# A decoder block on one core: x also laid out by features, the first norm's factors applied where projections leave PSUM, the front's weights laid out piece by piece

## The reference

```
xn   = x * rsqrt(mean(x*x, features) + 1e-6) * g_mix        # RMSNorm, one factor per token
proj = xn @ w_in     # q,k,v of attention A (4 x 128 columns each), q of B, six k/v groups of B
                     # (kcr, vcr, ks, vs, kw, vw: 128 columns each), 24 head gates, 2 x 1024 merge gates
# kcr and vcr: blocks of 32 tokens at stride 16 (31 of them), plus positions, flattened,
#              then gelu(. @ w1 + b1) @ w2  -> compressed keys and values
out1 = x + merge(attention_A, attention_B, gates) @ w_out
```

## Time and profile before

| | us |
|---|---|
| median of 3 executions | 1177.87 (1176.14 to 1178.73) |
| profiled execution | 1176.71 |
| its span, first to last instruction | 1174.9 |
| PE busy in the span | 1109.4 (94%) |
| DVE, ACT, POOL busy | 457.6, 286.4, 286.9 |

### The profile page before, as it was taken

The page is one execution under the profiler, slowest core; times in us unless marked ns, Lnnn a source line. Parts: engine busy times, 40 slices in busy tenths (PEclk is TensorE's granted clock), DMA queues, the critical chain, the costliest instruction groups (busy, mean ns, idle before and its releaser), DMA issues.

```text
span 1174.9 us, 19004 instructions
## 1 busy us (share of the span) xinstructions
PE 1109.4 (94%) x7570; PEld 654.2 (56%) x7571; DVE 457.6 (39%) x1026; ACT 286.4 (24%) x642; POOL 286.9 (24%) x215
## 2 busy tenths in 40 slices
PE   6999999999998989989999999999998899989796
PEld 5888787767776879654333433334343333433375
DVE  5244655545446733542223421212221211111787
ACT  5123333333336510031111111111111111111523
POOL 5522524342333520010111111111111112110043
PEclk9999999999999989989999999999999989989898
DMA  9921222221213430669999999999999999998771
GB/s 297 241 54 37 73 55 73 55 54 54 56 37 111 123 118 37 251 248 413 406 420 415 421 422 424 418 410 419 407 420 405 407 408 406 405 396 315 311 315 71
DMA packets 118072, 305.67 MB, mean 260 GB/s; under 512 B 21688, under 2 KB 79712, under 8 KB 92128
## 3 DMA queue, kind: packets, MB, share of 16 engines
q1 hardware_dynamic: 105856, 270.88, 60.3%
q0 software_dynamic: 12128, 33.57, 7.2%
HBM read 288.69 MB, written 26.21 MB: 268 GB/s over the span
## 4 chain that ended last, share of the span: by engine, by line
PE 72%; DMA 9%; SPq 7%; issue 6%; DVE 2%; POOLq 1%; POOL 1%; ACT 1%; DVEq 0%; ACTq 0%
PE bank L1467 17%; PE bank L457 16%; PE bank L1491 8%; DMA sb_gate_up<-in_w_up 7%; SPq L988 5%; PE bank L1083 4%; PE bank L1073 4%; PE bank L466 3%; PE bank L490 3%; PE bank L521 3%; DMA sb_down<-in_w_down 3%; PE bank L1457 2%; PE bank L503 2%; PE bank L1108 2%; SPq L992 2%
## 5 line engine op out<-in xcount | busy, mean ns | idle before, releaser
L1467 PE MATMUL bank<-sb_gate_up,sb_xgT 128*32 128x512 f32 (+2 forms) x2144 | 304.9, 610 | 19.3 <-DMA sb_gate_up<-in_w_up 19.3
L1467 PEld LDWEIGHTS bank<-sb_gate_up,sb_xgT 128*32 128x32 f32 (+2 forms) x2144 | 96.2, 119 | 196.1 <-issue 193.0
L457 PE MATMUL bank<-sb_x_hl,sb_w_hl 128*128 128x512 f32 x768 | 189.1, 398 | 1.0 <-DVE sb_x_hl L578 1.0
L457 PEld LDWEIGHTS bank<-sb_x_hl,sb_w_hl 128*128 128x128 f32 x768 | 140.4, 188 | 47.6 <-issue 17.0
L1491 PE MATMUL bank<-sb_down,sb_work 128*32 128x512 f32 (+2 forms) x1072 | 153.0, 595 | 2.8 <-DMA sb_down<-in_w_down 1.6
L1549 POOL DMA_INDIRECT expert_rows<-sb_rows_out,sb_work x42 | 43.3, 1032 | 459.6 <-DVE sb_rows_out L1627 439.9
L241 POOL TENSOR_TENSOR sb_w_hl<-sb_r,sb_w_hl 128x1024 fp32r<-128x1024 f32 x54 | 131.2, 2432 | 59.7 <-ACT sb_w_hl L1196 45.0
L1637 DVE TENSOR_TENSOR sb_work<-sb_work,bank 128x256 f32<-128x256 f32 x42 | 17.7, 423 | 274.3 <-ACT sb_work L1673 274.3
L1491 PEld LDWEIGHTS bank<-sb_down,sb_work 128*32 128x32 f32 (+2 forms) x1072 | 46.5, 116 | 79.2 <-issue 76.5
L1673 ACT ACTIVATE sb_work<-bank 128x256 f32<-128x256 f32 x42 | 16.2, 386 | 302.7 <-PE bank L1467 302.7
L656 DVE CUSTOM_DVE_ANT_0 sb_h<-bank,sb_bias 128x128 f32<-128x128 f32 (+3 forms) x96 | 43.3, 488 | 112.3 <-PE bank L490 111.8
(11 more groups left out here) (258 smaller groups left out, 1324.7 us busy)
## 6 DMA issues: line engine op xcount, KB each, us to landing
sb_gate_up<-in_w_gate SPq DMA_DIRECT2D x64, 1024.0 KB, 19.8
sb_gate_up<-in_w_up SPq DMA_DIRECT2D x64, 1024.0 KB, 27.9
sb_down<-in_w_down SPq DMA_DIRECT2D x64, 1024.0 KB, 28.8
sb_r<-in_w_in SPq DMA_DIRECT2D x34, 512.0 KB, 3.8
sb_rows<-expert_rows SPq DMA_DIRECT2D x6, 2048.0 KB, 16.3
sb_r<-in_w_out SPq DMA_DIRECT2D x8, 512.0 KB, 3.7
sb_rows<-expert_rows SPq DMA_DIRECT2D x3, 1024.0 KB, 8.7
sb_h<-in_x SPq DMA_DIRECT2D x4, 512.0 KB, 5.2
```

Of the source, the lines that this page charges most:

```text
L457: last = nc.tensor.matmul(out[:, :], w6_hl[:, slot_at[n], zw, k, :], x_hl[:, zx, k, :], start=k + i == 0, stop=k == KD - 1 and i == 2)
L1467: last = nc.tensor.matmul(bank[BH][rows, :], xgT[:, k, rows], gate_up[slot_of[r]][:, :, k, :], start=k == 0, stop=k == KD - 1)
```

## The change

Nothing of the arithmetic on weights changes; the layouts are made ahead of the launch. x_T is x by features, [128, 4096]; w_front holds every piece as [128, 1024], so that a partition's part is one run of 4 KB; the compression weights, biases and positions come ready laid out too. x_hl is now made of x_T times g, without the tokens' factors, and each factor is applied at eviction: by rbc, the factors spread over 128 partitions (for products by features), or by rr (for products by rows). rbc comes from a product of ones with four diagonal blocks.

```diff
 front_sync:
-            for t in range(NT): ... h[:, t] <- x tile t (identity after t == 1)
-            load_columns 0, 1; biases, positions; load_columns 2 to 4
+            load_piece(sp, 0)
+            x_by_features(0)                  # y[:, c] <- x_T, 512 KB each
+            load_piece(sp, 1)
+            for c in range(1, NT):
+                x_by_features(c)
+            load_piece(sp, 2)
+            for t in range(NT):
+                sp.dma_start(h[:, t, :], a["x"][0, t * P:(t + 1) * P, :]).then_inc(s_x[t], 16)
+            sp.dma_start(cst[:, 0:2 * P], a["cst"][:, 0:2 * P]).then_inc(s_ident, 16)
+            for n in range(3, 5):
+                load_piece(sp, n)
             ... head gates' weights; then b1, pos2, pos2x; rest of the constants; pieces 5, 6; w1[0]; w2; piece 7; w1[1]; ...
 front_gpsimd:
-            pool.dma_start(g_rows, ...)
+            pool.dma_start(g_col, a["g_mix_col"][:, :]).then_inc(s_g, 16)
-            for t in range(NT): wait s_ms; rr[t] = ...      (ahead of all pieces)
             for n in range(N_ACT_HI):
                 pool.wait_ge(s_w_hi, n + 1)
                 rest_of_piece(buf_of[n], slot_at[n])
+                if n == 2:
+                    for t in range(NT):
+                        pool.wait_ge(s_ms, t + 1)
+                        nc.gpsimd.tensor_tensor(rr[:, t:t + 1], ms[:, t:t + 1], C["nhalf"][:, 0:1], ALU.pow).then_inc(s_rr, 1)
 front_tensor:
-            transposes of g_rows, of y (32), of pos_rows
-                if j == 0 and f >= 2: pe.wait_ge(F["evicted"], f - 1)
+                out = bank_of(f)              # banks 0, 1, 6, 7 for f < 4, then BF[f % 2]
+                if j == 0 and f >= 4:
+                    pe.wait_ge(F["evicted"], bank_before.get(f, f - 2) + 1)      # {4: 0, 5: 1}
+                    if (f, j) == (2, 1):
+                        pe.wait_ge(s_ident, 16)
+                        pe.wait_ge(s_diag, 1)
+                        for t in range(NT):
+                            last = nc.tensor.matmul(bank[BS[0]][:, t * P:(t + 1) * P], C["ones"], diag[:, t, :], start=True, stop=True)
+                        last.then_inc(s_rbc, 1)
 front_vector:
+            dve.wait_ge(s_g, 16)
+            for k in range(KD):
+                dve.wait_ge(s_x_T[k // 2], 16)
+                dve.wait_ge(s_hi, k + 1)
+                nc.vector.scalar_tensor_tensor(out=x_hl[:, 1, k, :], in0=x_T[:, k, :], scalar=g_col[:, k:k + 1], in1=x_hl[:, 0, k, :].bitcast(F32), ...)
             for t in range(NT): norm_sums of h[:, t]        (now behind the low halves)
+            for t in range(NT):
+                dve.wait_ge(s_rr, t + 1)
+                last = nc.vector.tensor_scalar(diag[:, t, :], ident, rr[:, t:t + 1], None, ALU.mult)
+            last.then_inc(s_diag, 1)
+            dve.wait_ge(s_rbc, 1)
+            nc.vector.tensor_copy(rbc, bank[BS[0]][:, :])
 compress_blocks(i):
-                raw_kv = bank[BF[i]][:, :].rearrange("p (n t two) -> p two t n", t=8, two=2)
+                nc.vector.tensor_tensor(kv_normed[i], bank_of(i)[:, :], rbc, ALU.mult)
+                dve.drain()
+                raw_kv = kv_normed[i].rearrange("p (n t two) -> p two t n", t=8, two=2)      # SBUF
 evict(f): every copy becomes a tensor_tensor with rbc or rr, the scaling of q a scalar_tensor_tensor with rbc
 front_scalar:
-            for t in range(NT): y[:, t] = h[:, t] * rr
-                act.wait_ge(s_tp, k + 1)
-                nc.scalar.activation(x_hl[:, 0, k, :], bank[k][:, :], ACT.Copy, scale=g_col[:, k:k + 1]).then_inc(s_hi, 1)
+            round_first(0)
+                act.wait_ge(s_x_T[k // 2], 16)
+                nc.scalar.activation(x_hl[:, 0, k, :], x_T[:, k, :], ACT.Copy, scale=g_col[:, k:k + 1]).then_inc(s_hi, 1)
                 if k == 1: round_first(1)
             act.wait_ge(s_gn, 16)                           (as before)
             nc.scalar.copy(gn_hl[:, 0], gn_w).then_inc(s_hg, 1)
             for n in range(2, N_ACT_HI): round_first(n)     (as before)
```

More of the change, by code:

```diff
@@ L60 @@
 PASSES = ((0, 0), (0, 1), (1, 0))
+PIECES = [("kcr", COL_KCR), ("vcr", COL_VCR), ("q0", COL_QA), ("k0", COL_KA), ("v0", COL_VA), ("v1", COL_VA + P),
+          ("q1", COL_QA + P), ("k1", COL_KA + P), ("q2", COL_QA + 2 * P), ("k2", COL_KA + 2 * P), ("v2", COL_VA + 2 * P),
+          ("v3", COL_VA + 3 * P), ("q3", COL_QA + 3 * P), ("k3", COL_KA + 3 * P), ("ks", COL_KS), ("kw", COL_KW),
+          ("q4", COL_QB), ("vs", COL_VS), ("vw", COL_VW)]
+GATE_PIECES = [("g%d" % m, COL_GA + P * m) for m in range(2 * KD)]
@@ new lines, with by_partitions, layouts @@
+PIECES += GATE_PIECES[0:1] + [("q5", COL_QB + DH)] + GATE_PIECES[1:5] + [("q6", COL_QB + 2 * DH)] + GATE_PIECES[5:9]
+PIECES += [("q7", COL_QB + 3 * DH)] + GATE_PIECES[9:16]
+TWO_PARTS = ("q4", "q5", "q6", "q7")
+WO = [(0, 2), (3, 5), (1, 3), (2, 4), (4, 0), (5, 1), (6, 2), (7, 3)]
+def by_partitions(w):
+    k = w.shape[0] // P
+    return w.reshape(k, P, -1).transpose(1, 0, 2).reshape(P, -1)
+def layouts(inputs):
+    v = {n: np.asarray(inputs[n], np.float32) for n in _LAID_OUT}
+    w_in, w_out, wa, wb = v["w_in"][0], v["w_out"][0], v["w_branch_a"][0], v["w_branch_b"][0]
+    front = []
+    for name, c in PIECES:
+        cols = list(range(c, c + DH)) + list(range(c + 4 * DH, c + 5 * DH)) if name in TWO_PARTS else slice(c, c + P)
+        front.append(by_partitions(w_in[:, cols]))
+    heads = wb.reshape(2, 4, DH, D).transpose(0, 2, 1, 3).reshape(P, 4, D)
+    for m in range(KD):
+        cols = slice(m * P, (m + 1) * P)
+        front.append(np.concatenate([by_partitions(wa[:, cols]), heads[:, :, cols].reshape(P, -1)], axis=1))
+    for c, _ in WO:
+        front.append(by_partitions(w_out[:, c * P:(c + 1) * P]))
+    pos = np.concatenate([v["cmp_pos_" + n][0].reshape(16, P).T for n in "kv"], axis=1)
+    return {"w_front": np.stack(front),
+            "w_head_gates": by_partitions(w_in[:, COL_GN:COL_GN + 3 * NH]),
+            "x_T": by_partitions(v["x"][0].T),
+            "cmp_w1": np.stack([by_partitions(v["cmp_w1_" + n][0]) for n in "kv"]),
+            "cmp_w2": np.concatenate([v["cmp_w2_" + n][0].reshape(2, P, DH).transpose(1, 0, 2) for n in "kkv"], axis=2).reshape(P, -1),
+            "g_mix_col": np.ascontiguousarray(v["g_mix"][0].reshape(KD, P).T),
+            "cmp_cols": np.concatenate([v["cmp_b1_" + n][0].reshape(2, P).T for n in "kv"] + [pos], axis=1),
+            "cmp_pos_swapped": np.concatenate([pos[DH:], pos[:DH]], axis=0)}
@@ L175, in build @@
         s_w_hi = sem("s_w_hi")
[L178 to L184, removed]
+        pieces = PIECES
         WM_PIECE, WO_PIECE = 38, 46
@@ L189, in build @@
         SLOT_WM = [0, 1, 2, 5, 3, 4, 0, 1]
-        WO = [(0, 2), (3, 5), (1, 3), (2, 4), (4, 0), (5, 1), (6, 2), (7, 3)]
         SLOT_OF = SLOT_WM + [slot for _, slot in WO]
         buf_of = [n % 5 for n in range(54)]
-        two_loads = [PIECE["q%d" % i] for i in range(4, 8)]
         landed, so_far = [], [0] * 5
         for n, b_ in enumerate(buf_of):
-            so_far[b_] += 32 if n in two_loads else 48 if WM_PIECE <= n < WO_PIECE else 16
+            so_far[b_] += 16
             landed.append(so_far[b_])
@@ L213, in build, with load_piece @@
                 freed_by[n + 1] = max(freed_by[n], freed_by[n + 1])
-        def load_piece(sp, n, cols):
+        def load_piece(sp, n):
             if n >= 5:
                 sp.wait_ge(s_split, n - 4)
[L219 to L231, removed]
+            b_ = buf_of[n]
+            sp.dma_start(r1[:, 1024 * b_:1024 * (b_ + 1)], a["w_front"][n]).then_inc(s_rawp[b_], 16)
         def split_piece(pool, buf, slot):
@@ L266, in build @@
         gates = small[:, 0:96].rearrange("p (t n) -> p t n", t=NT)
-        g_rows, g_col = work[0:KD, 0:P], small[:, 436:436 + KD]
+        g_col = small[:, 436:436 + KD]
+        rbc = work[:, 6072:6584]
         ms, rr = small[:, 96:100], small[:, 100:104]
@@ L326, in build @@
         NF = len(products)
+        bank_of = lambda f: bank[(0, 1, 6, 7)[f] if f < 4 else BF[f % 2]]
+        bank_before = {4: 0, 5: 1}
         made = {}
@@ L377, in front_sync @@
[L377 to L385, removed]
@@ L394, in front_sync @@
-            sp.dma_start(w2[:, :, 2 * DH:3 * DH], a["cmp_w2_v"][0].rearrange("(c p) n -> p c n", p=P)).then_inc(s_w2, 16)
-            sp.dma_start(gpk[:, :], a["g_ple"][0].rearrange("(k p) -> p k", p=P), allow_slow_non_contiguous=True).then_inc(s_gpk, 16)
[L396 to L401, removed]
+                load_piece(sp, n)
@@ new lines, in front_sync @@
+            sp.dma_start(w1[0].rearrange("p t n -> p (t n)"), a["cmp_w1"][0]).then_inc(s_w1, 16)
+            sp.dma_start(w2.rearrange("p c n -> p (c n)"), a["cmp_w2"][:, :]).then_inc(s_w2, 16)
+            sp.dma_start(gpk[:, :], a["g_ple"][0].rearrange("(k p) -> p k", p=P), allow_slow_non_contiguous=True).then_inc(s_gpk, 16)
+            load_piece(sp, 7)
+            sp.dma_start(w1[1].rearrange("p t n -> p (t n)"), a["cmp_w1"][1]).then_inc(s_w1, 16)
```

(11 more changed lines are left out.)

102 lines of the change are left out of this document (29 added, 73 removed).

## The result

| kernel | median us (lowest to highest) | ratio to before, 95% interval |
|---|---|---|
| before, 7 executions beside it | 1177.86 (1176.14 to 1178.73) | |
| changed, 7 executions | 1182.19 (1179.51 to 1185.15) | 1.0043 (1.0028 to 1.0057) |
| changed, second comparison | 1184.09 (1182.82 to 1186.07) | 1.0061 (1.0047 to 1.0074) |
| changed, third comparison | 1182.23 (1180.05 to 1183.64) | 1.0045 (1.0027 to 1.0063) |

The change makes the kernel slower by 4.3 to 7.0 us, where about 9 were forecast. The profiled execution took 1185.15 us, 8.4 more than the profiled one of before; it is the slowest of the seven, so the medians and not the two profiles give the size.

The account below looks back on a forecast made before the run. TensorE was taken to bound the kernel, with 72% of the chain and no slack behind the front. Product 4's delay of 7.5 us plus 2.3 for the clock gave 9.8 on 1176.7, 1186.5, said as 1187; range 1173.5 to 1191.

Parts of the forecast that it names:

- Sign and cause: Front, eviction 0: slower, since block additions with two SBUF inputs alternate with POOL's instructions; product 4 starts 7.5 us later.
- The gate weights: SyncE's queue: the head gates' 96 KB land at 21.6 us (18.8 to 22.9), holding up piece 2's rounding.
- Turns: Eviction 0: eight additions of 0.4 us alternate with POOL's rests 4 to 8 and piece 8's cast, ending at 46.6 us.
- The gap before product 2: TensorE: product 1 ends at 23.0 us, product 2 waits for piece 2's rest until 25.5; gap 2.5 us.
- TensorE's start: Start of the front: without the transposes, TensorE could begin at about 8 us, once x_T tiles and piece 0 are split.
- The clock: TensorE at product 4: after the stall the clock is at 1.2 GHz; loss 1.7 to 3.4 us, 2.3 taken.
- Sum of the front: Late product 4 plus fall of the clock: 7.5 + 2.3 = 9.8 us, handed on to the end.
- The total: Whole kernel: 1186.5 us for the profiled execution, 1187 as median, with the front's loss handed on whole.
- likeliest case: Whole kernel: additions wait for POOL and the clock falls; 1183 to 1191 us, chance 0.54.
- rival 3: Front: same clash, milder, with piece 8 late, diagonal early, low clock loss; 3 to 6 us slower, 1181 to 1183.5, chance 0.11.
- rival 1: Eviction 0: additions run as now beside POOL, product 4 starts at 37.4 to 39.6; 1176 to 1180 us, chance 0.17.
- Rival 2: SyncE's queue: gate weights land before 15 us, additions meet one rest only; 4.2 us gained, 1173.7, chance 0.13.

Follow-up runs that it names:

- e1: Changed kernel, with the factor multiplied into the products in their PSUM bank and the block additions reading PSUM again; 1176.46 us, ratio to before 0.9994.
- e6: Changed kernel with one wait more: POOL holds the rest of piece 6 until evictions 0 and 1 are done; 1176.09 us, ratio to before 0.9990.
- b1: Kernel before, with kcr and vcr copied to SBUF and the block additions reading the copy; 1187.46 us, ratio to before 1.0086.
- e2: Changed kernel with the head gates' weights loaded behind piece 1, additions still in SBUF; 1181.45 us, ratio to before 1.0035.
- e5: e4 plus POOL waiting with the rest of piece 2 for the low halves and of piece 3 for the diagonal; 1171.42 us, ratio to before 0.9949.
- a1_third: Changed kernel, unaltered, measured and profiled a third time; 1182.23 us, ratio to before 1.0045.
- e4: e3 with g_mix's 4 KB loaded by SyncE ahead of piece 0 instead of by POOL; 1173.06 us, ratio to before 0.9968.
- a0_again: Changed kernel, unaltered, measured and profiled a second time; 1184.09 us, ratio to before 1.0061.
- b2: Kernel before, with only the new layouts of pieces, head gates' weights and first compression weights; 1177.88 us, ratio to before 1.0008.
- e3: Changed kernel with the additions reading PSUM (e1) and the head gates' weights loaded behind piece 1 (e2); 1175.39 us, ratio to before 0.9986.

## Why the prediction was right, and where its sizes were off

- **Sign and cause**: right. Slower; the eight additions of eviction 0 wait for POOL's rests by turns. e1 and e6 take away 7.6 us and 6.1 us against the changed kernel of their own comparison by moving only the additions' source or POOL's turn, and b1 makes such a loss (10.4 us) without the rest of the change.
- **The gate weights**: they were forecast to land at 21.6 and landed at 21.49; the ones matmuls were forecast near 30 and came at 29.96, product 4 at 46.7 and came at 45.47. The landing was in part luck. I took 7.04 MB at 361 GB/s; 351 GB/s were moved on average up to 21.49 us (323 from 2 to 7 us, 407 from 7 to 20), which is 7.5 MB, since transfers issued behind the gates moved too.
- **Turns**: I had three additions behind rests 5 to 7, one behind the cast and one behind rest 8. So it was, but POOL was through with rest 7 at 39.6 instead of 40.75 and piece 8 came 0.9 us later than forecast, and three slipped in between at 0.57. That is why product 4 came 1.2 us earlier than forecast.
- **The gap before product 2**: forecast were 2.5 us, and there was next to none: product 2 began at 26.27, right behind product 1, whose end I had at 23.0. The step that was mis-sized is TensorE's start, about 8 us forecast and 11.21 measured. The load of g on POOL's queue landed only at 7.9, and the high halves of x and POOL's first rest (8.17) both began then; I had written that this load had until 21.6. The first low half waited for that rest in its turn (2.27 us). A second error lies behind it. From 13.9 to 18.3 us the matmuls of product 0 came about every 0.43 us, and every 0.23 from then on; in the kernel before they came every 0.23 from the first. The windows below show it (6 and 11 matmuls in two us); the clock printed for both is 1.00, so the cause isn't shown. What is on record is that the kernel before had its transposes on TensorE ahead of product 0, and that the change takes them away. The diagonal, which was ready only at 29.8, hid both errors.

```profile
16.00:18.00 2.00, 2.00 (x6) 1.54 (x6) 2.00 (x4) 0.00 (x0) 0.00 (x0) 1.00 1.04 397
...
20.00:22.00 2.00, 2.00 (x11) 1.65 (x10) 2.00 (x5) 0.48 (x2) 0.00 (x0) 1.00 1.12 393
```

- **The clock**: forecast were 2.3 us. Products 4 and 5 took 13.32, 13.49 and 14.47 us in the three profiles instead of 11.67, that is 1.7 to 2.8 more, by the windows at a clock of 0.50 at first. e1 and e6 without the stall: 11.67 and 11.70.
- **Sum of the front**: 9.8 forecast (7.5 + 2.3), and 8.1, 8.5 and 9.0 at product 8 in the three profiles.
- **The total**: 1187 forecast, 1182.19 measured, which is below the likeliest case's own range (1183 to 1191) and in the place of rival 3, the clash in its mild form; the profiled execution (1185.15) lies in that range. The loss forecast was 9.1 us, and 4.3 were measured (7.0 and 5.2 in the later comparisons). The term that failed is the last one, that the front's loss is handed on whole: 3 us of 8 to 9 come back behind product 8 on average. In b1 it did hold (9.5 us late at product 8, 10.4 in the median), and in e2 to e5 within 1.4 us. About 1 us can be a small gain of the rest of the change: e1 and e6, whose fronts end within 0.3 us of the one of before, have medians 0.7 and 0.9 us under it, though both intervals hold 1. Another part goes with the clock. From product 8's end to the first expert matmul the twelve profiles took 458.3 to 463.5 us: 458.3 to 458.6 in the three with a mean clock of 0.96 from 360 to 540 us (a1_third, e4, e6), 460.6 to 461.5 in the three with 0.94 (before, a0_again, e2), 461.7 to 463.0 in the five with 0.93, and 463.5 in the one with 0.92, the first profile of the changed kernel. The windows of before, of this profile and of a1_third, in this order:

```profile
360.00:540.00 180.00, 167.90 (x1024) 133.25 (x1021) 93.86 (x191) 48.53 (x78) 44.29 (x27) 0.94 0.46 168
...
360.00:540.00 180.00, 168.28 (x1010) 135.57 (x1009) 95.55 (x198) 50.68 (x84) 43.64 (x27) 0.92 0.40 148
...
360.00:540.00 180.00, 168.00 (x1024) 133.42 (x1023) 97.56 (x203) 51.27 (x86) 44.86 (x27) 0.96 0.42 157
```

The profiles of one kernel differ in this as much as those of different kernels. The whole stretch behind product 8 varies by 6 us (1103.9 in e4 to 1110.4 in b2), so two single profiles can't tell the total closer than that. No run fixed the clock, and why the medians of the changed kernel give 3 us back stays open.

- **Rivals 1 and 2**: rival 1 (no clash) is refuted by the changed kernel's chain; e1, which takes the clash away, gives what rival 1 forecast (product 4 at 37.4 to 39.6, 1176 to 1180 us; it came at 39.03, 1176.46). Rival 2's trigger did not occur. e2 forces it alone and lost 4.3 us instead of gaining 4.2, since the additions of eviction 0 met the end of one rest and two whole ones, not one rest only. e3, which removes the clash of the additions as well, gained 1.7 us.

Two rules of the Trainium skill stood against each other here. That of the Trainium skill's "SBUF — State Buffer", Who interferes with whom, was right: the trace has 2.14 to 2.58 us for additions that take 0.57 with POOL idle. The Trainium skill's "VectorE: DVE Perf Modes", Rules for kernel authors, leaves two ways with a matmul's output, to work on it in PSUM or, before many operations, to copy it to SBUF first; the second cost 10.4 us in b1, where POOL was busy beside it.

## What to carry to other kernels

Before moving a VectorE operand from PSUM to SBUF, look whether the instruction then has two SBUF inputs and what GpSimd does at that time: beside GpSimd's back-to-back rests of 2.4 us each addition of 0.57 us took 2.1 to 2.6 us, because it waited for a whole rest. The additions are not the only ones: the low halves waited so too, and so did the fourth diagonal block (2.42 us instead of 0.29), which reads one tile and one factor per partition. The cure can be one wait: let GpSimd do later what nobody needs yet (e6, e5). And a small load that an in-order engine waits for (ACT, the gates) dams up all that stands behind it, so look at what lands ahead of it, and at how much work its landing sets free at once.

## What I had not expected

- **Strided SBUF reads are dearer than PSUM's.** With POOL idle eight additions out of SBUF take 4.74 us (0.59 each), out of PSUM 3.41 (0.43), same shape and pattern.
- **POOL waits for its own load.** In all seven profiles with g on POOL's queue its first rest began 0.25 us after ACT's first instruction that waits for g (7.92 and 8.17 in the changed kernel), though the rest has no use for g; with g on SyncE it began at once behind ACT. The drain behind the load is the likeliest cause; it was not tried alone.
- **4 KB rows ran faster than those of x had**: 407 GB/s between 7 and 20 us of the changed kernel (the last number of the window below), against the 361 that I took. The 323 GB/s from 2 to 7 us and the half MB of later transfers made up for it.

```profile
7.00:20.00 13.00, 7.72 (x21) 5.72 (x22) 11.21 (x11) 5.96 (x9) 5.12 (x2) 1.00 1.03 407
```
